# Attention's opening with sample work moved ahead of step 1, value fills from step 1, and later loads back from memory

## The chip, the cores and the metric

The kernel runs on one core of one Trainium2 chip. The metric is the device time of one execution in microseconds (us). A core has five engines that run at the same time, each through its own list of instructions: TensorE (PE: matmuls and transposes), VectorE (DVE), ScalarE (ACT), GpSimd (POOL) and SyncE (SP, which here only issues transfers). They wait for one another on semaphores. Transfers between the large memory and the on-chip buffers are issued from SP's queue (hardware queue, q1 in the profile) and POOL's queue (software queue, q0), and all run on the same 16 DMA engines.

## The reference, cut to what matters

One decoder layer for 1024 prompt tokens and 8 sample tokens. Between two feed-forward blocks stand an RWKV-7 branch and a differential attention with 4 heads of two maps each. What bears on the change is the attention:

```
def diff_attn_core(q, k, v, q_pos, k_pos, lam):
    s = jnp.einsum("bqhd,bkhd->bhqk", q, k).astype(F32) * (DA_QK ** -0.5)
    s = jnp.where(k_pos[None, :] <= q_pos[:, None], s, -jnp.inf)
    p = jax.nn.softmax(s, axis=-1).reshape(b, DA_HEADS, 2, tq, tk)
    w = p[:, :, 0] - lam * p[:, :, 1]
    return jnp.einsum("bhqk,bkhd->bqhd", w.astype(v.dtype), v)
...
        kp = cache_k[pt].reshape(n_past, 2 * DA_HEADS, DA_QK)
        vp = cache_v[pt].reshape(n_past, DA_HEADS, DA_V)
```

The prompt attends causally to itself, in blocks of 128 queries. Each of the 8 sample tokens attends to 2048 cached tokens, 16 pages of 128 tokens found through a page table, and to itself. A page of keys or values is 128 rows of 512 float32, 256 KB.

## The kernel before, in words

**Units.** Before attention, the input projection runs as 30 units (UNITS, numbers 0 to 29), 128 columns each: PE multiplies, DVE evicts the result from PSUM (L1922), ACT applies a sigmoid to a gate (L1382) and POOL saves it to memory (L931, gate_save). Into these units the sample's attention scores are woven: a *key group* f (0 to 31, four pages; group 4b to 4b+3 belongs to sample b) is loaded by SP into one of two slots of key_ring, and DVE multiplies it by the query (L1873) and sums it (L1877) into score_sums. GROUPS_OF says how many key groups each unit takes. SP issues the pages of group f after DVE's multiplication of group f-2 has freed the slot. When all 32 are done, DVE takes the maximum over each row (L1954), POOL the maximum over the partitions (L953).

**Steps.** Prompt attention is 27 steps (STEPS, numbers 0 to 26): step 0 takes the first query block with all 4 heads, steps 1 and 2 the second block with 2 heads each, then one head of one block per step. FIRST is 11: up to step 10 scores are made two steps ahead, later one. In a step PE makes scores of a later step (L2671), waits for this step's weights from DVE (the semaphore w_ready), transposes them (L2693), waits for ACT's copy of them (L1439), sums squares of the last output (L2677) and multiplies by the values (L2714). DVE's part of a step is to normalise the weights (L2023 to L2034; its end sets w_ready) and to find the maxima of a later step's scores (`maxima`, L2004 to L2007); ACT exponentiates (L1416).

**The sample's softmax** is woven in as three pieces on DVE (`sample_softmax`): piece 0 subtracts the maxima from the scores (L1965 to L1967), ACT exponentiates (`sample_exp`), piece 1 sums (L1970), PE sums over the partitions (`sample_sums`, L2635), piece 2 turns this into weights (L1974 to L1985).

**Fills.** A *fill* f (0 to 31) multiplies four value pages by the sample's weights on PE (L2647); FILL_STEP gives the step of each. Value pages go through a ring of three slots: SP issues the four pages of fill f when fill f-3 is done (the semaphore value_used), one page after the other, each with a page number read from the table (L701). The slot of f % 3 = 2 lies in tmp, so fill 2 also waits until all gates are saved. PE's order is fixed, so a fill whose pages have not landed holds up all that stands behind it. After the fourth fill of a sample its sum is moved, turned and added (`turn_sums`, `sample_out`).

**Loads back.** After the units, POOL issues the constants loop_masks (L954) and then 20 loads of 516 KB each, 10.57 MB together, of the RWKV operands kk, b_vec, k_new, r_mix and v_mix (L964). They are needed only after the last step. Their rows are 1032 float32 (4128 bytes) per partition, those of a value page 512 float32 (2048 bytes).

Of the kernel before, what the change touches and what calls it, by code (L numbers as in the profile page):

```python
# [11 lines left out]
AX = mybir.AxisListType.X  # L12
# [3 lines left out]
P = 128  # L16
# [3 lines left out]
NS = 8  # L20
# [16 lines left out]
PAGES = 16  # L37
# [94 lines left out]


UNITS = ZT + GT
GROUPS_OF = [0 if n == 0 else 2 if n in (15, 20, 26) else 1 for n in range(UNITS)]
HALF_OF = [n for n in range(UNITS) for _ in range(GROUPS_OF[n])]
PREP_AT = [4, 10, 16, 22]

# [90 lines left out]
def build(nc, A):  # L229

    ctx = ExitStack()
    with ctx:
        ev = Events(nc, ctx)
# [228 lines left out]
        AT_MERGE = AT_GATES + GT // 2  # L462
# [115 lines left out]
        BATCHES = [(0, range(0, 4)), (1, range(0, 2)), (1, range(2, 4))] + [(q, range(h, h + 1)) for q in range(2, 8) for h in range(HP)]  # L578
        STEPS = len(BATCHES)
        FIRST = 3 + 2 * HP  # L580
        FILL_STEP = [s for s in range(3, STEPS - 2) for _ in range(2 if s in (9, 11, 13, 14, 15, 18, 19, 20, 23, 24) else 1)]

        def heads_to(step):

# [191 lines left out]
        def _(pool):  # L776
# [132 lines left out]
            def spill_z(n):  # L909

                m = Z_ORDER[n]
                if m == 12 or 4 <= m < 8:
                    return
                pool.wait_ge(*ev.at("z_mixed", n + 1))
                if m == 13:
                    pool.wait_ge(*ev.at("z_act", 2))
                dst = gd_save if m == 13 else r_save[m] if m < 4 else v_save[m - 8]
                pool.dma_start(dst, ring[:, n % 2, :]).then_inc(ev[f"z_stored{n % 2}"], 16)

            for n in range(UNITS):  # L920
                p, s = n // 2, n % 2
                if n < ZT:
                    zm, z = z_place(n), T[:, s, :]
                    pool.wait_ge(*ev.at(f"psum_free{s}", AT_Z + p + 1))
                    pool.wait_ge(*ev.at("z_place", n + 1))
                    nc.gpsimd.tensor_tensor(zm[:, 1:NP], z[:, 0:NP - 1], z[:, 1:NP], ALU.subtract).then_inc(ev["z_diff"], 1)
                if 0 < n <= ZT:
                    spill_z(n - 1)
                if n >= ZT:
                    pool.wait_ge(*ev.at(f"gate_made{s}", p - ZPAIRS + 1))  # L930
                    pool.dma_start(g_save[n - ZT], T[:, s, :]).then_inc(ev[f"gate_saved{s}"], 16)  # L931
                for h in range(HP):
                    if PREP_AT[h] + 4 == n:
                        pool.wait_ge(*ev.at("cum_made", 2 * h + 2))
                        pool.dma_start(cum_save[h], cum).then_inc(ev["prep_stored"], 16)
                        pool.wait_ge(*ev.at("kk_made", h + 1))
                        pool.dma_start(kk_save[h], kkh).then_inc(ev["prep_stored"], 16)
                        pool.wait_ge(*ev.at("fac_made", h + 1))
                        nc.gpsimd.tensor_tensor(bh, bh, kkh, ALU.mult).then_inc(ev["b_made"], 1)
                        nc.gpsimd.tensor_tensor(kf[:, h, :], kf[:, h, :], fac, ALU.mult).then_inc(ev["kp_made"], 1)  # L940
                        pool.wait_ge(*ev.at("b_made", h + 1))
                        pool.dma_start(b_save[h], bh).then_inc(ev["prep_stored"], 16)
                        pool.wait_ge(*ev.at("kp_made", h + 1))
                        pool.dma_start(kp_save[h], kf[:, h, :]).then_inc(ev["prep_stored"], 16)
                if n == 16:
                    pool.wait_ge(*ev.at("side_moved", SIDE_AT["z_rows", 0, 0]))
                    pool.dma_start(A["shift_prompt"][0].rearrange("b (m p) -> (b m) p", p=P), zrow[0:ZT, :])\
                        .then_inc(ev["z_rows_stored"], 16)
                    pool.dma_start(A["shift_sample"][0].rearrange("b (m p) -> (b m) p", p=P), zrow[ZT:9 * ZT, :])\
                        .then_inc(ev["z_rows_stored"], 16)  # L950

            pool.wait_ge(*ev.at("s_max_part", 1))
            nc.gpsimd.partition_all_reduce(smax, smaxp, P, bass.bass_isa.ReduceOp.max).then_inc(ev["s_max_all"], 1)  # L953
            pool.dma_start(masks, A["const_table"][:, CONST_AT[LOOP_CONSTS]:NCONST]).then_inc(ev["masks_loaded"], 16)  # L954
            pool.wait_ge(*ev.at("unit_done0", AT_MERGE))
            pool.wait_ge(*ev.at("unit_done1", AT_MERGE))
# [1 line left out]
            pool.wait_ge(*ev.at("z_stored0", 16 * ring_before(ZT)))  # L958
            pool.wait_ge(*ev.at("z_stored1", 16 * ring_before(ZT + 1)))
            pool.wait_ge(*ev.at("z_rows_stored", 32))  # L960
            for dst, src, done in ((KKn, kk_save, "kk_back"), (Bf, b_save, "b_back"), (Kf, kp_save, "kp_back"),
                                   (Rf, r_save, "r_back"), (Vf, v_save, "v_back")):
                for h in range(HP):
                    pool.dma_start(dst[:, h, :], src[h]).then_inc(ev[done], 16)  # L964
# [140 lines left out]
        def _(act):  # L1105
# [312 lines left out]
            def decays(c):  # L1418
# [8 lines left out]
                    last = sc.activation(Pinv[:, h, :], CUMX[h][:, c, 1:C + 1], ACT.Exp, scale=-LOGDECAY)  # L1427
                last.then_inc(ev["ck_p"], 1)

            probs(0)  # L1430
            for step in range(STEPS):
                s, (qi, group) = (step + 1) % 2, BATCHES[step]
                if step + 1 < FIRST:
                    probs(step + 1)
                act.wait_ge(*ev.at("w_trans_lo", step + 1))
                if step >= FIRST:
                    act.wait_ge(*ev.at("w_trans_hi", step + 1 - FIRST))
                n = (qi + 1) * P * len(group)
                sc.activation(wT[s][:, 0:n], PSf[:, 4 * 512:4 * 512 + n], ACT.Copy).then_inc(ev["w_moved"], 1)  # L1439
                if FIRST <= step + 1 < STEPS:  # L1440
                    probs(step + 1)
                if step == STEPS - 2:
                    act.wait_ge(*ev.at("cum_back0", 16))
                    act.wait_ge(*ev.at("gate_saved0", 8 * GT))
                    act.wait_ge(*ev.at("gate_saved1", 8 * GT))
                    act.wait_ge(*ev.at("value_used", 4 * NS))
                    decays(0)
                act.wait_ge(*ev.at("o_done", step + 1))
                out = PS[:, 6, 0:len(group) * P]
                sc.activation(Q[:, group[0]:group[-1] + 1, qi * P:(qi + 1) * P], out.rearrange("p (h n) -> p h n", n=P), ACT.Copy)  # L1450
                if opens_block(step):
                    sums = PS[:, 5, 0:P] if qi < 3 else PS[:, 6, P:2 * P]
                    sc.activation(rmix[:, (qi - 1) * P:qi * P], sums, ACT.Copy, scale=1.0 / P).then_inc(ev["o_rows"], 1)
                if step == STEPS - 1:
                    sc.activation(rmix[0:96, qi * P:NP], PS[0:96, 6, P:2 * P], ACT.Copy, scale=1.0 / P)
                sc.activation(osq[:, 0:len(group) * P], out, ACT.Square).then_inc(ev["o_moved"], 1)
                if step == 0:
                    sample_exp()
                for b in range(NS):
                    if FILL_STEP[4 * b + 3] == step:  # L1460
                        act.wait_ge(*ev.at("value_used", 4 * b + 4))
                        sc.activation(osum, PS[:, 7, :], ACT.Copy).then_inc(ev["osum_moved"], 1)
# [136 lines left out]
        def _(dve):  # L1599
# [3 lines left out]
            def in_turn(instruction):  # L1603


                dve.drain()
# [301 lines left out]
            def unit_keys(h):  # L1908

                dve.wait_ge(*ev.at("side_moved", SIDE_AT["back", h, 2]))  # L1910
                in_turn(v.tensor_tensor(kkh, kkh, fac, ALU.mult).then_inc(ev["kk_made"], 1))

            q_diag(0)
            split(1, AT_Z)
            for n in range(UNITS):
                p, s = n // 2, n % 2
                c = AT_Z + p
                dve.wait_ge(*ev.at(f"unit_done{s}", c + 1))
                if p > ZPAIRS:
                    dve.wait_ge(*ev.at(f"gate_saved{s}", 16 * (p - ZPAIRS)))  # L1920
# [24 lines left out]
                for h in range(HP):  # L1945
# [3 lines left out]
                        inverse_norms(h)  # L1949
                    if PREP_AT[h] + 3 == n:  # L1950
                        unit_keys(h)

            smx = smaxp.rearrange("p (b m) -> p b m", b=NS)
            in_turn(v.tensor_reduce(smx, SC.rearrange("p (b g m) -> p b m g", b=NS, g=PAGES), AX, ALU.max)\  # L1954
                .then_inc(ev["s_max_part"], 1))

            def pages(a):

# [50 lines left out]
            def o_inverse(qi):  # L2009
# [3 lines left out]
                in_turn(v.tensor_scalar(rmix[:, b], rmix[:, b], 0.0, EPS, ALU.max, ALU.add))  # L2013
                in_turn(v.reciprocal(rmix[:, b], rmix[:, b]).then_inc(ev["o_inverse"], 1))

            maxima(0)
            maxima(1)
            sample_softmax(0)
            for step in range(STEPS):
                s, (qi, group) = (step + 1) % 2, BATCHES[step]  # L2020
                k, n, (_, total, inv, _) = len(group), (qi + 1) * P, softmax_columns(step)
# [14 lines left out]
                    maxima(step + 2)  # L2036
                if FIRST <= step + 1 < STEPS:
                    maxima(step + 1)
                if 0 < step < 3:
                    sample_softmax(step)  # L2040
                for b in range(NS):
                    if FILL_STEP[4 * b + 3] == step - 1:
                        sample_out(b)
# [316 lines left out]
        def _(pe):  # L2360
# [263 lines left out]
                    turn_rows(2 * HP - 1)  # L2624
            pe.wait_ge(*ev.at("side_moved", NSIDE))
            pe.wait_ge(*ev.at("psum_free0", AT_MERGE))
            pe.wait_ge(*ev.at("psum_free1", AT_MERGE))
            pe.wait_ge(*ev.at("k_back", 16))
            pe.wait_ge(*ev.at("q_back", 16))

# [46 lines left out]
                    mm(PS[32 * h:32 * h + 1, bank, at:at + P], K("ones")[:, 0:1], osq[:, i * P:(i + 1) * P], start=True, stop=True)  # L2677

            scores(0)
            scores(1)  # L2680
            for step in range(STEPS):
                s, (qi, group) = (step + 1) % 2, BATCHES[step]
# [2 lines left out]
                    scores(step + 2)  # L2685
                if FIRST <= step + 1 < STEPS:
                    scores(step + 1)
                if step == 2:
                    sample_sums()
                pe.wait_ge(*ev.at("w_ready", step + 1))  # L2690
                pe.wait_ge(*ev.at("w_moved", step))
# [382 lines left out]
```

## Time and profile before

| | us |
|---|---|
| median of 3 runs | 2707.53 |
| lowest, highest | 2707.19, 2708.59 |
| the profiled execution, whole | 2708.69 |
| its span on the core | 2707.0 |
| attention, first scores to the end of the last step's product | 1283.9 to 1485.0 |

The span is what the trace covers, and all moments below count from its start. PE is busy for 96% of the whole span, but the share hides that attention is different: the views by stretch below give busy time per engine inside it, with the clock that the throttle granted to TensorE (1.00 is 2.4 GHz, 0.50 is 1.2 GHz) and what the DMA engines moved. A row of the timeline is: start, duration, engine, line, operation, output <- input, and in brackets how long the engine sat idle before it and what ended that wait.

### The profile page before, as it was taken

The page shows a single profiled execution, that of the slowest core. Times are in us where ns is not written, and L with a number is a line of the kernel's source. Part 1 is how long each engine was busy: PE and PEld are TensorE (multiplying, and loading weights), DVE is VectorE, ACT ScalarE, POOL GpSimd, SP SyncE. Part 2 cuts the span into 40 slices and gives each one's busy share as a digit, 9 for nine tenths or more (in the row PEclk, how much of TensorE's full clock was granted, in tenths as well). Part 3 has the DMA queues.
Part 4 walks back from the last instruction along what each step waited for, and adds up shares of the span by engine and source line. Part 5 has one row for each costly group of instructions (what it writes and reads, how often), then busy time and mean ns, then how long its engine had stood idle before and what let it go on. Part 6 is the DMA issues. An engine that isn't in the chain of part 4 may idle for free.

```text
span 2707.0 us, 55005 instructions
## 1 busy us (share of the span) xinstructions
PE 2595.5 (96%) x22506; PEld 2464.0 (91%) x22506; DVE 1709.3 (63%) x2054; ACT 802.3 (30%) x1306; POOL 592.4 (22%) x534
## 2 busy tenths in 40 slices
PE   7999999999999999998787999979999999999998
PEld 7999999999999999998344899869999999999998
DVE  5877777422484588677766778675487677763223
ACT  6333333111211222332444233221343333331012
POOL 2333332100010232111100655220023333320000
PEclk8999999999999999999799999979999999999999
DMA  5233332751323545667876000043323333235411
GB/s 196 73 116 98 110 107 64 272 182 55 102 95 106 157 142 171 220 203 251 287 223 184 30 27 28 20 147 109 125 75 111 106 99 112 73 106 203 153 47 71
DMA packets 293398, 342.12 MB, mean 126 GB/s; under 512 B 22324, under 2 KB 217744, under 8 KB 293024
## 3 DMA queue, kind: packets, MB, share of 16 engines
q1 hardware_dynamic: 252960, 189.42, 23.6%
q0 software_dynamic: 40000, 149.17, 15.2%
q8 instruction: 176, 2.88, 0.4%
q14 instruction: 70, 0.57, 0.1%
q10 hardware_dynamic: 192, 0.07, 0.0%
HBM read 254.32 MB, written 84.28 MB: 125 GB/s over the span
## 4 chain that ended last, share of the span: by engine, by line
PE 86%; DVE 7%; issue 2%; SPq 1%; DMA 1%; ACT 1%; DVEq 0%; POOL 0%; ACTq 0%
PE ps L2384 42%; PE ps L2512 31%; PE ps L2752 1%; PE ps L2767 1%; PE ps L2772 1%; PE ps L2429 1%; PE ps L2714 1%; DVE small L2006 1%; SPq L700 1%; PE ps L2671 1%; PE ps L2604 1%; DMA q_rot<-q_save 1%; PE ps L2647 1%; PE ps L2799 1%; SPq L701 1%
## 5 line engine op out<-in xcount | busy, mean ns | idle before, releaser
L2384 PE MATMUL ps<-h,w_hi 128*128 128x344 f32 x2112 | 506.4, 323 | 0.0
L2384 PEld LDWEIGHTS ps<-h,w_hi 128*128 128x128 f32 x2112 | 361.9, 188 | 17.4 <-issue 16.7
L2384 PE MATMUL ps<-h,w_lo 128*128 128x344 f32 x1056 | 336.7, 319 | 0.0
L1766 DVE SCALAR_TENSOR_TENSOR x_res<-ps,x_res 128x1032 f32<-128x1032 f32 x48 | 59.2, 1233 | 322.0 <-PE ps L2384 322.0
L2512 PE MATMUL ps<-t,w_hi 128*128 128x258 f32 x1408 | 259.3, 285 | 0.0
L1182 ACT ACTIVATE w_hi<-w_stage 128x512 fp32r<-128x512 f32 x252 | 157.6, 627 | 315.9 <-PE ps L2512 279.8
L2512 PE MATMUL ps<-t_one,w_hi 128*128 128x258 f32 x1280 | 234.3, 284 | 3.1 <-issue 2.5
L2512 PEld LDWEIGHTS ps<-t,w_hi 128*128 128x128 f32 x1408 | 219.9, 191 | 0.0
L1708 DVE TENSOR_TENSOR tmp<-tmp,ps 128x516 f32<-128x516 f32 x210 | 145.4, 692 | 106.8 <-PE ps L2512 93.7
L1677 DVE TENSOR_TENSOR w_lo<-w_stage,w_hi 128x512 fp32r<-128x512 f32 x252 | 192.0, 762 | 22.7 <-ACT w_hi L1182 0.4
L2512 PEld LDWEIGHTS ps<-t_one,w_hi 128*128 128x128 f32 x1280 | 198.9, 190 | 3.4 <-issue 3.4
L2512 PE MATMUL ps<-t,w_lo 128*128 128x258 f32 x704 | 199.9, 284 | 0.0
L2384 PEld LDWEIGHTS ps<-h,w_lo 128*128 128x128 f32 x1056 | 198.3, 188 | 0.0
L2512 PE MATMUL ps<-b,w_hi 128*128 128x258 f32 x1056 | 192.7, 283 | 0.0
L2512 PE MATMUL ps<-t_one,w_lo 128*128 128x258 f32 x640 | 181.2, 283 | 0.0
L2512 PE MATMUL ps<-h,w_hi 128*128 128x258 f32 x960 | 174.8, 283 | 1.4 <-ACT tmp L1206 0.8
L2512 PEld LDWEIGHTS ps<-b,w_hi 128*128 128x128 f32 x1056 | 163.3, 189 | 0.0
L809 POOL TENSOR_TENSOR w_stage<-w_stage 128x512 f32<-128x512 f32 x42 | 76.7, 1827 | 344.5 <-DVE w_lo L1677 336.6
L2512 PEld LDWEIGHTS ps<-h,w_hi 128*128 128x128 f32 x960 | 148.3, 189 | 1.9 <-issue 1.8
L2512 PE MATMUL ps<-b,w_lo 128*128 128x258 f32 x528 | 149.1, 282 | 0.0
L1192 ACT ACTIVATE w_hi<-w_stage 128x1024 fp32r<-128x1024 f32 x49 | 51.7, 1056 | 285.1 <-PE ps L2384 266.5
L2512 PE MATMUL ps<-h,w_lo 128*128 128x258 f32 x480 | 135.4, 282 | 0.0
(551 smaller groups left out, 6161.1 us busy)
## 6 DMA issues: line engine op xcount, KB each, us to landing
w_stage<-in_ffn_up SPq DMA_DIRECT2D x176, 256.0 KB, 3.0
key_ring<-in_cache_k SPq DMA_DIRECT2D x128, 256.0 KB, 3.0
value_ring<-in_cache_v SPq DMA_DIRECT2D x88, 256.0 KB, 3.0
w_stage<-in_w_in SPq DMA_DIRECT2D x84, 256.0 KB, 3.4
w_stage<-in_ffn_down SPq DMA_DIRECT2D x80, 256.0 KB, 3.3
g_save<-g_ring POOLq DMA_DIRECT2D x32, 516.0 KB, 4.8
g_save<-g_kept POOLq DMA_DIRECT2D x32, 516.0 KB, 4.4
x_res<-x_save POOLq DMA_DIRECT2D x6, 2064.0 KB, 9.3
```

Of the source, the lines that this page charges most:

```text
L700: page = sp.value_load(ptab[0:1, at], min_val=0, max_val=N_PHYS - 1)
L701: sp.dma_start(slot, cache[ds(page, 1)].rearrange("a t n -> (a t) n")).then_inc(ev[done], 16)
L809: nc.gpsimd.tensor_tensor(A12, A12, A11, ALU.subtract).then_inc(ev[of(m, "sum_made")], 1)
L1182: sc.activation(op_slot(whi, n), RAW[i], ACT.Copy).then_inc(ev[of(m, "op_high")], 1)
L1192: sc.activation(whi[b], stg[b], ACT.Copy).then_inc(ev[f"w_high{b}"], 1)
L1677: in_turn(v.tensor_tensor(op_slot(wlo, n), RAW[n % NPROD], op_slot(whi, n).bitcast(F32), ALU.subtract) .then_inc(ev[of(m, "op_low")], 1))
L1708: in_turn(v.tensor_tensor(halved(out), halved(x), region(bank), ALU.add).then_inc(ev[of(m, "ps_read")], 1))
L1766: in_turn(v.scalar_tensor_tensor(ch3(xm), dense[s], 0.5, ch3(xm), ALU.mult, ALU.add) .then_inc(ev[f"psum_free{s}"], 1))
L2006: in_turn(v.tensor_reduce(top, scores, AX, ALU.max))
L2384: last = mm(dense[s][:, j], w[w0][:, k0 + k, :], column(r, k, slice(j * CH, (j + 1) * CH)), start=(k == 0 and n == 0), stop=(k == nk - 1 a ...
L2429: last = mm(dense[s][:, j], w[s][:, k, :], r[:, k, j * CH:(j + 1) * CH], start=(k == 0 and n == 0), stop=(k == KT - 1 and n == 2))
L2512: last = mm(PS[:, bank + c, 0:QUART], w[:, k, :], moving[:, x, k, b], start=(opens and k == 0 and a == 0), stop=(k == 3 and a == 2), skip_ ...
```

## The change

In words:

1. GROUPS_OF: unit 29 has no key group, unit 27 has two instead of one. Groups 29 and 30 are now multiplied in unit 27, group 31 in unit 28. DVE takes the row maximum at the head of unit 29, ahead of that unit's eviction, and POOL the maximum over partitions in unit 29, ahead of the save of the last gate.
2. sample_softmax: piece 0 ahead of the maxima of steps 0 and 1, piece 1 behind them, piece 2 in step 0 (before: piece 0 behind those maxima, piece 1 in step 1, piece 2 in step 2). sample_exp stands ahead of the first exponentials, and PE's sample_sums in step 0 instead of step 2.
3. FILL_STEP: sample b has one fill in step 3b+1, two in step 3b+2 and one in step 3b+3, from step 1 to step 24. Before, fills ran from step 3 to step 24: one a step, and two in steps 9, 11, 13, 14, 15, 18, 19, 20, 23 and 24.
4. POOL issues the 20 loads back only when step 5 has been transposed (w_trans_lo reaches 6). Before, it did so right after the maximum over partitions.
5. PE waits for the eviction of unit 29 only ahead of the scores of step 1, no longer ahead of those of step 0.

```
-GROUPS_OF = [0 if n == 0 else 2 if n in (15, 20, 26) else 1 for n in range(UNITS)]
+GROUPS_OF = [0 if n in (0, UNITS - 1) else 2 if n in (15, 20, 26, 27) else 1 for n in range(UNITS)]
...
-        FILL_STEP = [s for s in range(3, STEPS - 2) for _ in range(2 if s in (9, 11, 13, 14, 15, 18, 19, 20, 23, 24) else 1)]
+        FILL_STEP = [3 * b + k for b in range(NS) for k in (1, 2, 2, 3)]
...
+                if n == UNITS - 1:
+                    pool.wait_ge(*ev.at("s_max_part", 1))
+                    nc.gpsimd.partition_all_reduce(smax, smaxp, P, bass.bass_isa.ReduceOp.max).then_inc(ev["s_max_all"], 1)
...
-            pool.wait_ge(*ev.at("s_max_part", 1))
-            nc.gpsimd.partition_all_reduce(smax, smaxp, P, bass.bass_isa.ReduceOp.max).then_inc(ev["s_max_all"], 1)
...
+            pool.wait_ge(*ev.at("w_trans_lo", 6))
             for dst, src, done in ((KKn, kk_save, "kk_back"), (Bf, b_save, "b_back"), (Kf, kp_save, "kp_back"),
...
+            sample_exp()
             probs(0)
...
-                if step == 0:
-                    sample_exp()
...
+                if n == UNITS - 1:
+                    in_turn(v.tensor_reduce(smx, SC.rearrange("p (b g m) -> p b m g", b=NS, g=PAGES), AX, ALU.max)
+                            .then_inc(ev["s_max_part"], 1))
                 dve.wait_ge(*ev.at(f"unit_done{s}", c + 1))
...
+            sample_softmax(0)
             maxima(0)
             maxima(1)
-            sample_softmax(0)
+            sample_softmax(1)
...
-                if 0 < step < 3:
-                    sample_softmax(step)
+                if step == 0:
+                    sample_softmax(2)
...
-            pe.wait_ge(*ev.at("psum_free1", AT_MERGE))
...
             scores(0)
+            pe.wait_ge(*ev.at("psum_free1", AT_MERGE))
             scores(1)
...
-                if step == 2:
+                if step == 0:
                     sample_sums()
```

**How the order moves.** On DVE, from the end of the units to the opening of attention, before:

```order
L1922 TENSOR_TENSOR tmp<-ps,rstd_mix 128x1032
L1873 TENSOR_TENSOR kq_prod<-key_ring,rstd 128x2048
L1877 TENSOR_REDUCE score_sums<-kq_prod 128x32
L1954 TENSOR_REDUCE rstd<-score_sums 128x64
L2004 TENSOR_TENSOR ps<-ps,const 128x1024
L2006 TENSOR_REDUCE rstd<-ps 128x8
L2007 TENSOR_SCALAR rstd<-rstd 128x8
L2004 TENSOR_TENSOR ps<-ps,const 128x4x128
L2006 TENSOR_REDUCE rstd<-ps 128x4
L2007 TENSOR_SCALAR rstd<-rstd 128x4
L1965 TENSOR_TENSOR rstd<-rstd,s_self 128x64
L1966 TENSOR_TENSOR score_sums<-score_sums,rstd 128x1024
```

and now (line numbers are up to 5 higher; L1921 is the row maximum, L1966 to L1968 are piece 0):

```order
L1874 TENSOR_TENSOR kq_prod<-key_ring,rstd 128x2048
L1878 TENSOR_REDUCE score_sums<-kq_prod 128x32
L1921 TENSOR_REDUCE rstd<-score_sums 128x64
L1927 TENSOR_TENSOR tmp<-ps,rstd_mix 128x1032
L1966 TENSOR_TENSOR rstd<-rstd,s_self 128x64
L1967 TENSOR_TENSOR score_sums<-score_sums,rstd 128x1024
L1968 TENSOR_TENSOR s_self<-s_self,rstd 128x64
L2005 TENSOR_TENSOR ps<-ps,const 128x1024
L2007 TENSOR_REDUCE rstd<-ps 128x8
L2008 TENSOR_SCALAR rstd<-rstd 128x8
L2005 TENSOR_TENSOR ps<-ps,const 128x4x128
```

The last key group and the maximum went ahead of the last eviction, and piece 0 went ahead of the first maxima.

On PE, in steps 1 and 2 (from the transposes of step 1 to the scores made in step 3), before:

```order
L2693 MATMUL ps<-const,probs 128x128 x4
L2677 MATMUL ps<-o_squares,const 1x128 x4
L2714 MATMUL ps<-w_trans_105,v_tok 128x128 x4
L2671 MATMUL ps<-k_rot,q_rot 128x384 x2
L2635 MATMUL ps<-rstd,const 128x64
L2693 MATMUL ps<-const,probs 128x128 x4
L2677 MATMUL ps<-o_squares,const 1x128 x2
L2714 MATMUL ps<-w_trans_106,v_tok 128x128 x4
L2671 MATMUL ps<-k_rot,q_rot 128x384 x2
```

and now:

```order
L2695 MATMUL ps<-const,probs 128x128 x4
L2678 MATMUL ps<-o_squares,const 1x128 x4
L2716 MATMUL ps<-w_trans_105,v_tok 128x128 x4
L2648 MATMUL ps<-value_ring,s_weights 4x512 x4
L2672 MATMUL ps<-k_rot,q_rot 128x384 x2
L2695 MATMUL ps<-const,probs 128x128 x4
L2648 MATMUL ps<-value_ring,s_weights 4x512 x4
L2648 MATMUL ps<-tmp,s_weights 4x512 x4
L2678 MATMUL ps<-o_squares,const 1x128 x2
L2716 MATMUL ps<-w_trans_106,v_tok 128x128 x4
L2672 MATMUL ps<-k_rot,q_rot 128x384 x2
```

Three fills (L2648) entered these two steps, and the partition sum (L2635) left for step 0.

## Rows read from the trace of the kernel before

**Rows 1.** The page: the span.

```profile
span 2707.0 us, 55005 instructions
```

**Rows 2.** By stretch: PE, PEld, DVE, ACT, POOL busy; clock, DMA share, GB/s.

```profile
1284.00:1320.00 36.00, 21.92 (x97) 14.06 (x97) 29.36 (x52) 14.27 (x53) 11.55 (x22) 0.55 0.99 384
1320.00:1365.00 45.00, 38.16 (x248) 19.49 (x252) 30.13 (x69) 20.52 (x61) 0.00 (x0) 0.91 0.68 202
```

**Rows 3.** Timeline of SP and PE at attention's opening: the query load, the first scores.

```profile
1268.00 0.51 SPq L721 DMA_DIRECT2D q_rot<-q_save  x1
...
1283.89 3.38 PE L2671 MATMUL ps<-k_rot,q_rot 64*128 64x128 f32 x24 [7.29 <-DMA q_rot<-q_save]
```

**Rows 4.** Timeline of DVE and POOL: last key groups, the two maxima.

```profile
1259.71 2.29 DVE L1873 TENSOR_TENSOR kq_prod<-key_ring,rstd 128x2048 f32<-128x2048 f32 x1
...
1277.96 2.29 DVE L1873 TENSOR_TENSOR kq_prod<-key_ring,rstd 128x2048 f32<-128x2048 f32 x1
...
1282.71 1.99 DVE L1954 TENSOR_REDUCE rstd<-score_sums 128x64 f32<-128x1024 f32 x1
...
1288.12 0.54 POOL L953 PARTITION_ALL_REDUCE rstd<-rstd  x1 [8.24 <-issue]
```

**Rows 5.** Timeline of DVE: pieces 0, 1, 2 begin; weights of steps 1 and 3.

```profile
1291.59 1.23 DVE L1966 TENSOR_TENSOR score_sums<-score_sums,rstd 128x1024 f32<-128x1024 f32 x1
...
1300.56 0.69 DVE L2029 TENSOR_TENSOR probs<-probs 128x512 f32<-128x512 f32 x1
...
1303.40 2.00 DVE L1970 TENSOR_REDUCE rstd<-score_sums 128x64 f32<-128x1024 f32 x1
...
1310.59 0.22 DVE L1974 TENSOR_TENSOR rstd<-rstd,ps 128x64 f32<-128x64 f32 x1
...
1318.24 0.62 DVE L2034 SCALAR_TENSOR_TENSOR probs<-probs,small 128x384 f32<-128x384 f32 x1
```

**Rows 6.** Timeline of PE in steps 2 and 3.

```profile
1307.08 1.65 PE L2671 MATMUL ps<-k_rot,q_rot 64*128 64x384 f32 x4
...
1309.15 1.06 PE L2693 MATMUL ps<-const,probs 128*128 128x128 f32 x4
...
1311.42 2.08 PE L2714 MATMUL ps<-w_trans,v_tok 128*128 128x128 f32 x8
...
1318.91 0.90 PE L2693 MATMUL ps<-const,probs 128*128 128x128 f32 x3 [3.83 <-DVE probs L2034]
...
1322.50 1.89 PE L2647 MATMUL ps<-value_ring,s_weights 128*4 128x512 f32 x8
```

**Rows 7.** Fills: what ended waits before L2647; timeline of SP and PE, steps 11, 15.

```profile
  DMA value_ring<-in_cache_v: 5.2, 5
  DMA tmp<-in_cache_v: 3.2, 3
...
1364.39 1.90 PE L2647 MATMUL ps<-value_ring,s_weights 128*4 128x512 f32 x16
...
1388.40 3.61 SPq L701 DMA_DIRECT2D tmp<-in_cache_v  x4
...
1394.43 1.04 PE L2647 MATMUL ps<-tmp,s_weights 128*4 128x512 f32 x8 [0.86 <-DMA tmp<-in_cache_v]
```

**Rows 8.** DMA queues: packets, MB, engine share in 1328-1330, 1292-1294, 576-578; a load's landing.

```profile
q1 hardware_dynamic: 266, 0.49, 84.2%
...
q0 software_dynamic: 140, 0.53, 70.4%
q1 hardware_dynamic: 124, 0.24, 32.0%
...
q0 software_dynamic: 172, 0.71, 89.6%
q1 hardware_dynamic: 172, 0.08, 14.1%
...
v_mix<-v_save POOLq DMA_DIRECT2D x4, 516.0 KB, 20.1
```

More of the change, by code:

```diff
@@ L1911, in unit_keys @@
                 in_turn(v.tensor_tensor(kkh, kkh, fac, ALU.mult).then_inc(ev["kk_made"], 1))
+            smx = smaxp.rearrange("p (b m) -> p b m", b=NS)
             q_diag(0)
@@ L1951, in _ @@
                         unit_keys(h)
-            smx = smaxp.rearrange("p (b m) -> p b m", b=NS)
-            in_turn(v.tensor_reduce(smx, SC.rearrange("p (b g m) -> p b m g", b=NS, g=PAGES), AX, ALU.max)\
-                .then_inc(ev["s_max_part"], 1))
             def pages(a):
```

## The prediction

> **What bounds the kernel now.** Attention fills 1283.9 to 1485.0 us of the 2707.0 us span [rows 1, 3]; the change touches only it and the 25 us ahead of it, so I read the busy time by stretch first. In the opening (1284 to 1320) DVE is busy 29.4 of 36 us, PE 21.9, and the clock granted is 0.55, so nearly all of PE's work runs at 1.2 GHz; from 1320 to 1365 PE is busy 38.2 of 45 us at a clock of 0.91 [rows 2]. So the opening belongs to DVE, the rest to PE. Then the timelines, for what ends PE's waits. The first scores start at 1283.89 behind the query load, issued at 1268.00 [rows 3]. PE's last long wait in the opening, 3.83 us, ends with the weights of step 3 at 1318.9 [rows 6]. Third, the fills: eight waits on value pages, 8.4 us together [rows 7]. They show a second limit. Fill 17's four pages are issued from 1388.40 and its product starts at 1394.43: 6.0 us from a free slot to use, and SP issues a page in 1.09 us (3.61 us from the first issue to the end of the fourth, so 1.09 apart), hence a fill in 4.36 us at best. The last view is the DMA queues in windows of 2 us [rows 8]: alone, SP's queue moves 0.49 MB in 2 us, that is 240 GB/s, the rate of 1 MB per 4.36 us.
>
> **Units 27 to 29: no gain, none lost.** SP issues group 31's pages when group 29's multiplication is over, at 1262.0 [rows 4], and that row has nothing ahead of it that moves. So the keys come no sooner, and the query load behind them in SP's queue keeps its 1268.0. What moves is DVE work: groups 30 and 31 (2.3 + 2.3 us each) and the maximum (1.99) run back to back from 1264.5 with two evictions of 1.3 between them: 1264.5 + 4.7 + 1.3 + 4.7 + 2.0 = 1277.2. Unit 29's eviction slips by some 0.6 us; what waits for it is the scores of step 1, after 1284, so it costs nothing. POOL's maximum ended at 1288.66 and its input was ready at 1284.7 [rows 4]: 4.0 us, now 1277.2 to 1281.2. The last gate's save waits behind it, about 2 us later; who waits is fill 2's pages, not used before step 2. Bound for the first scores: 1 us sooner (less beside the query load) to 0; I take 0, the query load is what they wait for.
>
> **The opening: DVE's gain is handed back.** Piece 0 (1.9 us from 1291.3) [rows 5] goes into the wait for the queries, piece 1 (2.0 us) takes its place: step 0 is unmoved, its weights ready at 1296.0 as before. Piece 2 (1310.6 to about 1315.8, 5.2 us, [rows 5]) now stands between the weights of steps 0 and 1: those of step 1, at 1301.25 before [rows 5], come at 1306.5. From there PE needs transposes, ACT's copy, squares and product, 4.35 us as in step 2 (1309.15 to 1313.50) [rows 6]: 1310.9. Then fill 0 at the slow clock (1.9 us) and the scores for step 4 (1.65 us) [rows 6]: 1314.5. DVE waits for these, needs 1.7 us for their maxima (1308.8 to 1310.5, just ahead of piece 2) and 3.0 us for the output's inverse and the weights of step 3 (from piece 2's end at 1315.8 to 1318.86) [rows 5]: 1319.2, where it was 1318.9 [rows 5]. PE meanwhile does step 2 with fills 1 and 2 (3.8 us at the slow clock) and is some 5 us behind at step 3, less once its clock is up, with four fills done by step 3's end where it had one. I put the whole opening at +1 us in time and three fills ahead (bounds: -2 if the denser PE gets the full clock sooner, +4 if not).
>
> **The fills: more of them early, against the same rate.** Every three steps now take four fills. In steps 3 to 10 a step took 4 to 6 us, so four fills want to run in about 15 us, and SP needs 17.4 us to issue them. Fill 0 ends at 1312.9; SP then issues without a pause, and fill 6 lands at about 1333. At the full rate fill 14, the last of step 11, lands at 1333 + 8 x 4.36 = 1368; before, step 11 ended its second fill (the eleventh, not the fifteenth) at 1366.3 [rows 7]. So even undisturbed the value stream alone is 1.7 us behind there, plus 1 us for the fill itself: +2.7.
>
> **The loads back: the term that decides.** 10.57 MB are issued at step 5's transposes, near 1331, into a stretch where SP's queue is wanted at its full 240 GB/s. Before, they ran from 1289 to 1319 (the last four land 20.1 us after 1298 to 1300) [rows 8], when at most one fill's pages were in flight. What two full queues do is in the trace: from 576 to 578 they move 172 packets each, 0.71 and 0.08 MB, since packets of POOL's queue are 4128 bytes and those of the weights 512; the packets alternate. From 1292 to 1294, with the last value pages of the opening beside the first loads back, it is 140 against 124 packets, 0.53 against 0.24 MB [rows 8]. So value pages get 120 GB/s, not 240, while POOL's queue gets 265, for 10.57 / 0.265 = 40 us. In these 40 us 4.8 MB of pages arrive, 4.6 fills instead of 9.2. Fill 14 then lands at 1333 + 38 + (8 - 4.4) x 4.36 = 1387, its product ends at 1388, 22 us behind 1366.3. The bounds of this term: an equal share by bytes (192 GB/s each of the 384 in [rows 2]) gives 5.5 us per fill and 1377, 12 us behind; no loss at all gives 1369, 2.7 behind. I take the 22, because the row of 1292 shows this very pair of transfers.
> The Trainium skill, "DMA: Bandwidth & Descriptors", on arbitration, says that an engine round-robins between queue rows packet by packet, one packet being some 9 to 17 descriptors; that speaks against this change. A value page and a load back both give 8 rows to each engine, so by it value pages would get a third, 128 GB/s, and fill 14 would be 1 us sooner than by the row.
>
> **Behind step 11.** From step 12 the change has 17 fills where before had 21: 4 x 0.95 = 3.8 us less on PE (a fill is 1.04 at the full clock) [rows 7]. The steps are 6.5 to 8 us there and want at most 1.33 fills each, so SP keeps up, and waits such as the 0.86 before fill 17 [rows 7] go; I count 2 us of the 8.4. Against it, long waits on pages in steps 6 to 11 would leave PE at 1.2 GHz there, as in the opening [rows 2]; PE's work between the waits then takes up to twice as long, partly inside them: 0 to +5 us, I take +1.5. The end of attention: +22 - 3.8 - 2 + 1.5 = +17.7, with the opening already in the moment of fill 6. Nothing behind attention moves: the loads back are done near 1371, a hundred us before they are wanted. The profiled execution, 2708.7, would be 2726.4; on the median of 2707.5 that is **2725.2**.
>
> **Rivals.**
> *A. Pages starve, as above* (0.70). Term bounds: 12 to 24 us at step 11, so +7 to +24 at the end: 2714 to 2732.
> *B. The loads back slip in* (0.16). SP's queue alone leaves some 145 of 384 GB/s, and if value pages kept at least half by bytes, the loss at step 11 is 3 to 12 us, and the 5.8 us behind it give most of that back: -3 to +6, middle +2, 2709.5. For it: DMA share in 1320 to 1365 is only 0.68 [rows 2]. Against it: the 0.24 MB of 1292. To this case belongs that the change doesn't do what it says, since key pages do not come sooner.
> *C. Faster* (0.14). The mechanism is the even spread: value pages hold 4.36 us a fill beside the loads back, all 8.4 us of waits on pages vanish, and a PE that never waits long keeps 2.4 GHz where [rows 2] show 0.91. That gives 2.7 - 3.8 - 8.4 + 2 (waits that arise early) = -7.5, with clock up to -10: 2697 to 2701, I take 2700. It decides at about 215 GB/s for SP's queue in 1331 to 1371; below that fill 14 is over 5 us late and eats it.
>
> **Chances.** What a measurement here can tell from no change is about 0.2%, 5.4 us: 2702 to 2713. From A nearly all is slower; of B some 0.03 is slower and 0.13 same; C is faster by nine parts in ten. Slower 0.73, same 0.14, faster 0.13. The range for 8 in 10 reaches down to the middle of B and up past A's +24 by what a slow clock may add: 2704 to 2734.
>
> **What would show it.** In the profile after: the first scores still at 1283.9; step 3's weights near 1319; the queues from 1331 to about 1371 with SP's at 0.24 MB in 2 us and POOL's at 0.53; waits of PE before L2648 on value pages of well over 8.4 us, nearly all before 1390, and after it almost none; attention ending near 1503. If SP's queue keeps 0.45 MB in 2 us beside POOL's, the decisive term is wrong, and B or C holds. If step 3's weights come at 1315 or sooner, the opening was mis-walked.

## The result and the profile after

The changed kernel takes **2723.5 us** in the median of five runs (2720.8 to 2726.1), beside 2707.5 for the kernel before: a ratio of **1.0059, 95% interval 1.0045 to 1.0074**, so 16 us slower. The forecast was 2725.2.

The profiled execution has a span of 2721.4 us, against 2707.0 [rows 1]. Everything ahead of attention stands some 2.5 us earlier on its clock: the first eviction that the change leaves in its place (L1927 here, L1922 before) starts at 1254.55 us instead of 1257.06. So I count from the start of the first scores, 1280.53 here and 1283.89 before [rows 3]. Attention then lasts to 1499.15, the end of its last output product, which is 218.6 us, where it lasted 201.1. The whole loss lies there: from attention's end to the span's it is 1222.2 us here and 1222.0 before.

The same stretches as in [rows 2] and two more, of the kernel after (columns: busy time of PE, PEld, DVE, ACT, POOL, then granted clock, DMA share, GB/s):

```profile
span 2721.4 us, 55005 instructions
...
1284.00:1320.00 36.00, 23.00 (x130) 12.47 (x128) 28.56 (x54) 15.43 (x58) 0.00 (x0) 0.75 0.37 122
1320.00:1365.00 45.00, 22.36 (x124) 9.56 (x124) 18.73 (x42) 10.48 (x33) 10.59 (x20) 0.79 0.99 368
1365.00:1400.00 35.00, 29.60 (x201) 17.08 (x201) 20.84 (x50) 15.09 (x40) 0.00 (x0) 0.93 0.75 242
1400.00:1485.00 85.00, 72.19 (x481) 41.69 (x478) 62.95 (x125) 39.59 (x84) 0.00 (x0) 0.96 0.54 165
```

From 1320 to 1365 PE does 124 matmuls in 22.4 us, where it did 248 in 38.2; the DMA engines, 0.99 busy in the opening and 0.68 here before, are now 0.37 busy in the opening and 0.99 here. The POOL column holds the 20 issues. Two lines of the DMA queues say what that does, the first pair from 1342 to 1344, the last line from 1368 to 1370, when the loads back are over (packets, MB, share of 16 engines):

```profile
q0 software_dynamic: 146, 0.54, 67.2%
q1 hardware_dynamic: 146, 0.27, 35.7%
...
q1 hardware_dynamic: 413, 0.76, 102.7%
```

SP's queue has 135 GB/s beside POOL's and 380 as soon as it is alone (with some pages in arrears). The price is in PE's timeline, the fills that wait and fill 14:

```profile
1325.57 2.13 POOL L966 DMA_DIRECT2D kk<-kk_save  x4 [43.92 <-PE ps L2695]
...
1332.95 1.89 PE L2648 MATMUL ps<-value_ring,s_weights 128*4 128x512 f32 x8 [7.00 <-DMA value_ring<-in_cache_v]
1341.79 1.04 PE L2648 MATMUL ps<-value_ring,s_weights 128*4 128x512 f32 x8 [3.80 <-DMA value_ring<-in_cache_v]
1357.48 1.89 PE L2648 MATMUL ps<-value_ring,s_weights 128*4 128x512 f32 x8 [5.15 <-DMA value_ring<-in_cache_v]
1365.32 1.89 PE L2648 MATMUL ps<-value_ring,s_weights 128*4 128x512 f32 x8 [5.95 <-DMA value_ring<-in_cache_v]
...
1385.25 1.04 PE L2648 MATMUL ps<-tmp,s_weights 128*4 128x512 f32 x8
```

Three of the four long waits end with a fill at 1.89 us, nearly twice the 1.04 that it takes at 2.4 GHz: PE came out of the wait at 1.2. In all, PE's own waits on pages are 23.0 us (waits: total, times, longest), of before 2.2:

```profile
PE ps L2648 <- DMA value_ring<-in_cache_v: 22.4, 5, 7.0
PE ps L2648 <- DMA tmp<-in_cache_v: 0.6, 2, 0.3
...
PE ps L2647 <- DMA value_ring<-in_cache_v: 1.3, 2, 0.7
PE ps L2647 <- DMA tmp<-in_cache_v: 0.9, 1, 0.9
```

The chain of waits names PE for 85% of the whole span and the value pages for 1%. That looks like nothing, but 1.1% of 2721 us is 30 us: two stretches of 10.92 and 18.39 us, from 1330.82 and 1346.89, both while the loads back run (the chain counts the transfer's time there, not only PE's idle time). A share of the whole span hides what the same chain shows in a window.

### The profile page after: what moved, and what is told of

Same layout as the page of the kernel before. It is cut to its first block, busy times and chain, and to the rows that moved or that the text cites. A ratio compares the mean times of both kernels' runs of the same rounds, so it can differ in the third digit from the quotient of the medians.

```text
span 2721.4 us, 55005 instructions
## 1 busy us (share of the span) xinstructions
PE 2591.4 (95%) x22506; PEld 2458.6 (90%) x22506; DVE 1710.0 (63%) x2054; ACT 802.3 (29%) x1306; POOL 592.4 (22%) x534
## 4 chain that ended last, share of the span: by engine, by line
PE 85%; DVE 9%; DMA 3%; issue 1%; ACT 1%; SPq 1%; DVEq 0%; POOL 0%; ACTq 0%
PE ps L2386 41%; PE ps L2514 30%; PE ps L2754 1%; DMA value_ring<-in_cache_v 1%; PE ps L2769 1%; PE ps L2774 1%; PE ps L2431 1%; PE ps L2716 1%; DVE small L2007 1%; PE ps L2606 1%; PE ps L2801 1%; PE ps L2672 1%; PE ps L2648 1%; DVE kq_prod L1874 1%; PE ps L2809 1%
## 5 line engine op out<-in xcount | busy, mean ns | idle before, releaser
L2514 PE MATMUL ps<-t,w_lo 128*128 128x258 f32 x704 | 200.1, 284 | 0.0
L2514 PE MATMUL ps<-b,w_hi 128*128 128x258 f32 x1056 | 192.7, 283 | 0.0
```

The source lines that it names most:

```text
L2514: last = mm(PS[:, bank + c, 0:QUART], w[:, k, :], moving[:, x, k, b], start=(opens and k == 0 and a == 0), stop=(k == 3 and a == 2), skip_ ...
```

## Experiments: which part costs

The change has three parts: (1) the loads back behind step 5's transposes; (2) the table of fills; (3) key groups and sample softmax earlier. Theory S: all is (1), through the shared engines. The rival: the table costs or gains by itself.

**The wait that makes the loads back late, taken out of the change (e1), and put alone on the kernel before (e2).**

```diff
-            pool.wait_ge(*ev.at("w_trans_lo", 6))    # e1: out of the changed kernel
+            pool.wait_ge(*ev.at("w_trans_lo", 6))    # e2: into the kernel before
```

> The changed kernel without POOL's new wait, so the 20 loads back start right behind the maximum over partitions, as before the change; fills and sample softmax stay as changed. Theory S (value pages starve beside the loads back): the loads are done by about 1317, when SP has just begun to refill value slots; PE's waits on value pages before step 12 fall from about 22 us to under 6, fill 14 is used near 1366 instead of 1386, and the time is 2704 to 2710 us. Rival F (the new table of fills is the cost, since four fills in three short steps want more than SP can issue): the time stays at 2716 or more, and the waits on pages stay above 12 us.

Measured: 2707.7 us, 1.0001 (0.9992 to 1.0011) of before; attention 201.6 us.

> The kernel before with one line of the change: POOL waits for the transposes of step 5 ahead of the loads back. Theory S: from 1328 to 1368 value pages get 0.27 MB in 2 us instead of 0.49, 20 us of their stream are lost, the old fills had at most 2 us to spare between steps 11 and 15, so the time is 2722 to 2728 us with the last fill of step 15 near 1412. Rival F: the old table spares enough, 2708 to 2713 us.

Measured: 2722.7 us, 1.0055 (1.0038 to 1.0071); attention 214.3 us. The waits of PE on pages, of the first and of the second kernel:

```profile
PE ps L2647 <- DMA value_ring<-in_cache_v: 7.9, 3, 4.1
PE ps L2647 <- DMA tmp<-in_cache_v: 1.8, 1, 1.8
...
PE ps L2648 <- DMA value_ring<-in_cache_v: 10.5, 4, 6.6
PE ps L2648 <- DMA tmp<-in_cache_v: 5.5, 2, 4.1
```

One wait on POOL, which is 22% busy, carries the loss: 15.8 us taken away, 15.0 put on. In the traces, attention is 17.0 us shorter without it (218.6 and 201.6), and 13.3 of these are PE's waits on pages (23.0 and 9.7); the other 3.7, of which fills at the lower clock behind a wait are a part, were not taken apart. The 9.7 us of waits left in the first kernel are more than the 6 that were expected; they are the table's, as the next runs show.

**The table, with the loads late and with them early.**

```diff
-        FILL_STEP = [3 * b + k for b in range(NS) for k in (1, 2, 2, 3)]
+        FILL_STEP = [s for s in range(3, STEPS - 2) for _ in range(2 if s in (9, 11, 13, 14, 15, 18, 19, 20, 23, 24) else 1)]
```

> The changed kernel with the old table of fills (from step 3, two in ten of the steps); the late loads back stay. Theory S: as slow as the changed kernel or up to 4 us slower, 2721 to 2728 us, since the value stream starts later into the same 40 us of shared engines. Rival F: the table was the cost, 2708 to 2713 us.

Measured: 2718.3 us, 1.0042 (1.0025 to 1.0059); PE's waits on pages 18.0 us. That is below theory S's range and above the rival's.

> The changed kernel with both undone, the old table of fills and the early loads back: what is left are the key groups one unit sooner and the sample softmax ahead of step 1. Theory S and the walk of the opening: step 3's weights within 2 us of where they were, no starving, 2703 to 2708 us. If the opening's piece 2 in step 0 costs what it saves, it is 2707.5 to within 1 us.

Measured: 2703.9 us, 0.9986 (0.9976 to 0.9995); PE's waits 2.6 us, attention 197.3. So the table costs 5.2 us with the loads late and 3.8 with them early, and part (3) alone gains 3.8. By medians: -3.8 for the earlier softmax and key groups, +3.8 for the table, +15.8 for the loads, together +15.8, beside the +16.0 that was measured. The two small parts stand only just clear of the scatter: e4's interval against before allows a gain of 1.4 to 6.5 us, and the single runs of e1 (2706.5 to 2709.6) and e4 (2700.7 to 2708.4) overlap. For the table the traces say the same as the times: PE's waits on pages are 5.0 us shorter without it when the loads are late, and 7.1 when they are early. The loads' part is 14.4 to 15.8 in the three pairs, so it hardly depends on the table.

## Experiments: is it the place, the bytes or the burst

**Later, and only half of them.**

```diff
-            pool.wait_ge(*ev.at("w_trans_lo", 6))
+            pool.wait_ge(*ev.at("w_trans_lo", 17))           # e6
...
+                    if done == "kp_back" and h == 2:         # e7, in the loop of the loads
+                        pool.wait_ge(*ev.at("w_trans_lo", 6))
```

> The changed kernel with POOL waiting for the transposes of step 16 (w_trans_lo at 17) instead of step 5. Theory S with the step length in it: from step 16 a step takes 8 us and wants 1.33 fills, one in 6 us, while a fill takes 8 us beside the loads back; in 41 us 6.8 fills are wanted, 4.9 arrive and two are in the ring ahead, so most of the loss is covered: 2708 to 2716 us. Rival (the loads back cost the same wherever they run beside value pages): 2720 us or more.

Measured: 2718.5 us, 1.0046 (1.0029 to 1.0063), between the two ranges: the cost is smaller there than at step 5, but two thirds of it are left (10.8 us over e1, of 15.8). From 1422 to 1424, 25 us after POOL's first issue, the queues read

```profile
q0 software_dynamic: 141, 0.52, 65.4%
q1 hardware_dynamic: 141, 0.26, 34.7%
```

and the last fill to wait in that stretch waits 6.79 us, at 1439.31. I had thought that the longer steps there leave SP room. In e1 a step takes 7.4 us from step 16 to 21 and wants 1.33 fills, one in 5.6 us: that leaves SP 1.2 us a fill at its full rate of 4.36, and none at a third of the engines.

> The changed kernel with the wait for step 5's transposes put in front of the second ten of the 20 loads back; the first ten start right behind the maximum. Theory S: the shared stretch is 20 us instead of 41 and loses 2.3 fills instead of 4.7, so fill 14 is used 10 us sooner than in the changed kernel: 2711 to 2717 us, midway between the early loads (2707.7) and the changed kernel (2723.5). Rival T (a threshold: any loads back after step 5 spoil PE's clock or its order for good): 2720 us or more.

Measured: 2713.1 us, 1.0017 (1.0007 to 1.0026): 5.4 us over e1 for half of the bytes, where all cost 15.8. PE's waits on pages are 12.6 us, 2.9 over e1, where the whole burst adds 13.3. So the cost grows faster than the bytes. That the ring of pages takes the first part of a burst would explain it; no run tests that.

**Paced.** The same 20 loads in the same kernel, one behind each of the steps 5 to 24:

```diff
-            pool.wait_ge(*ev.at("w_trans_lo", 6))
+            i = 0
...
                 for h in range(HP):
+                    pool.wait_ge(*ev.at("w_trans_lo", 6 + i))
                     pool.dma_start(dst[:, h, :], src[h]).then_inc(ev[done], 16)
+                    i += 1
```

> The change, with GpSimd's 20 loads back issued one behind each of the steps 5 to 24 instead of all behind step 5. The bytes and the work are the same. While both queues run the engines move some 400 GB/s (0.79 MB in 2 us in the changed kernel), with the pages alone 245. A step of 5 us then has to bring one fill (1.05 MB) and one load (0.53 MB), 1.6 MB, which 400 GB/s bring in 4 us. Theory S (the cost is a burst that takes two thirds of the engines for 41 us while the fills are needed at their full rate): PE's waits on pages fall from 23 us to 2-8 and the time to 2706-2713. Rival B (any loads back during attention cost by their bytes, wherever they stand: 10.6 MB at 245 GB/s would be 43 us of engine time, of which the changed kernel paid 15.8): 2718-2724 as in the kernel with the loads at step 16.

Measured: **2707.1 us, 1.0000 (0.9991 to 1.0009)**; attention 200.1 us. Below, its row for 1320 to 1365, two of the twenty issues, and the queues' totals from 1330 to 1460:

```profile
1320.00:1365.00 45.00, 32.37 (x214) 16.32 (x213) 25.81 (x60) 16.29 (x51) 3.37 (x7) 0.92 0.90 299
...
1352.35 0.54 POOL L967 DMA_DIRECT2D b_vec<-b_save  x1 [4.94 <-PE ps L2697]
1358.39 0.54 POOL L967 DMA_DIRECT2D b_vec<-b_save  x1 [5.50 <-PE ps L2697]
...
q1 hardware_dynamic: 14291, 26.01, 61.5%
q0 software_dynamic: 2598, 9.53, 21.3%
...
PE ps L2650 <- DMA value_ring<-in_cache_v: 8.4, 3, 6.3
PE ps L2650 <- DMA tmp<-in_cache_v: 1.8, 1, 1.8
```

The same bytes inside attention cost nothing that can be measured against e1 (2707.1 and 2707.7), and PE's waits are again those of e1 (10.2 and 9.7 us). 9.5 MB of loads and 26.0 MB of pages passed in 130 us. So neither the bytes nor a place inside attention cost by themselves; the burst does, which for 41 us in a row holds SP's queue below what the fills want (where the burst stands matters some: 10.8 us at step 16, 15.8 at step 5). The rival by bytes is out.

**The size of the rows.** The engines take turns by packets, so smaller rows on POOL's queue should leave more to SP's. (The counts that later waits on these loads expect are raised to match.)

```diff
-                    pool.dma_start(dst[:, h, :], src[h]).then_inc(ev[done], 16)
+                    for q in (slice(0, HALF), slice(HALF, NT)):        # e5; e10: four quarters
+                        pool.dma_start(dst[:, h, q], src[h][:, q]).then_inc(ev[done], 16)
```

> The changed kernel with each load back cut into two of 128 x 516, so that POOL's queue carries packets of 2064 bytes beside value pages' 2048; bytes and moment are the same. Theory S, with packets of the two queues taken in turn: value pages get half of the bytes, near 0.38 MB in 2 us instead of 0.27, the loads back take some 55 us instead of 41, fill 14 is used about 10 us sooner than in the changed kernel, and the time is 2710 to 2717 us. Rival Q (the queues share by bytes or by a fixed weight, whatever the packet): 0.27 MB in 2 us as in the changed kernel and 2721 to 2726 us.

Measured: 2728.8 us, 1.0075 (1.0058 to 1.0092). No gain at all: outside what either theory had expected, above it. The lines of the queues, 1342 to 1344, show why the premise failed:

```profile
q0 software_dynamic: 157, 0.52, 67.5%
q1 hardware_dynamic: 150, 0.27, 37.9%
```

The share is the old one. POOL's queue moves 3.3 kB a packet: a transfer brings each engine 8 rows of 2064 bytes, 16.5 kB, and with one small packet at its end that fits four packets of 4128 bytes (4/5 of 4128 is 3.30), not eight of 2064 (8/9 of it would be 1.83). Two rows had been put in one packet. The row size was not the packet size, so the experiment changed nothing but the number of issues; attention is 219.5 us, as in the changed kernel (218.6). The two medians are 5.3 us apart, and the intervals overlap. Of the 6.8 us between the two profiled spans 2.9 lie ahead of attention, 0.9 in it and 3.0 behind it, so the loads' share of the engines does not explain them; the cause stays open.

> The change, with the loads back written as 80 transfers of 128 rows of 1032 bytes instead of 20 of 4128. In the kernel with 40 transfers of 2064-byte rows the trace has GpSimd's queue at 3.3 kB a packet (five packets for the 16.5 kB that a transfer brings to each engine, one of them small), not at 1.8: two rows went in one packet, and the two queues still took turns packet by packet, 0.25 to 0.14 MB in 1 us. Theory K (turns by packets, and the software queue fills a packet up to some 4.1 kB): here 3 packets for 8.3 kB, so 2.75 kB a packet on average; 240 packets an engine instead of 180, the shared stretch grows from 41 to some 52 us, at 2.75 to 1.8 kB; PE's waits on pages 23-30 us, time 2724-2733. Rival R (a packet is a row, as for the pages of the other queue): under 1 kB a packet, the pages get over 60 per cent of the bytes, PE's waits 5-15 us, time 2710-2720.

Measured: 2721.2 us, 1.0055 (1.0041 to 1.0068); attention 215.7 us; PE's waits on pages 20.9 us. The queues, 1342 to 1344, and the 80 issues' first group:

```profile
q0 software_dynamic: 159, 0.43, 60.0%
q1 hardware_dynamic: 159, 0.29, 42.4%
...
1325.53 8.60 POOL L967 DMA_DIRECT2D kk<-kk_save  x16 [44.01 <-PE ps L2696]
```

0.43 MB in 159 packets is 2.70 kB each, near the 2.75 of theory K (two of 4128 and a small one for 8.3 kB), and the two queues again have 159 packets each. Rival R, a packet to a row, is out. But the time is 3 us below K's range, and so are the waits (K: 23 to 30); the interval overlaps that of the changed kernel. The shared stretch did grow, to the 52 us of K (1325.5 to 1377), at 0.29 MB in 2 us for SP's queue instead of 0.27. What K left out is the start: POOL needs 43 us to issue 80 transfers at 0.54 us, and from 1326 to 1334 its queue brings 1.11 MB and SP's 1.30, where the changed kernel has 1.64 and 0.91. Whether this start is the whole of the difference was not tested.

**The table by measured rates.** Loads early, the changed kernel's opening, and fills that begin at step 2 and are spread with the aim that none is wanted sooner than SP's rate allows:

```diff
-        FILL_STEP = [3 * b + k for b in range(NS) for k in (1, 2, 2, 3)]
+        FILL_STEP = [2, 3, 4, 4, 6, 7, 8, 8, 10, 11, 11, 12, 13, 13, 14, 14, 15, 16, 16, 17, 18, 18, 19, 19, 20, 20, 21, 22, 23, 23, 24, 24]
-            pool.wait_ge(*ev.at("w_trans_lo", 6))
```

> The early loads back with another table of fills, one a step or less until step 10 and two in twelve of the later steps (from step 2 to step 24), with the sample softmax of the change. Theory S: fills should never be wanted faster than one in 4.4 us nor all come early; the waits on value pages fall below 2 us and PE has fewer long gaps: 2698 to 2704 us, faster than before. Rival: the table is worth nothing beyond the old one, 2703 to 2706 us.

Measured: **2700.8 us, 0.9976 (0.9967 to 0.9986)**: 7 us faster than the kernel before, 23 than the changed one. Its row and its waits:

```profile
1320.00:1365.00 45.00, 37.23 (x256) 19.86 (x256) 32.19 (x74) 21.82 (x63) 0.00 (x0) 1.00 0.72 209
...
PE ps L2647 <- DMA value_ring<-in_cache_v: 4.1, 4, 1.7
```

The waits are 4.1 us where under 2 were expected. In this execution PE keeps the full clock from 1320 to 1365, as in no other profiled one here, and attention takes 192.7 us. But it is one of the best three of its ten runs (2695.9 to 2696.7, with a mean granted clock of 0.980 to 0.981 over the whole run); the other seven took 2700.5 to 2705.1 at 0.976 to 0.977, so the row shows the kernel at its best and not at its median. Over e4 the gain is 3.2 us, and the two intervals against before overlap: that this table beats the old one is likely but not shown. Whether the 3.2 us come from fills in steps 2 to 4, from fewer in late steps or from the clock was not taken apart.

## Why the prediction was right, and where its steps were not

**The decisive term held, for its reason.** Fill 14's product ends 105.8 us behind the first scores (1386.29 - 1280.53); before, step 11 ended 82.4 behind them: +23.4, where the working had +22. SP's queue had 0.27 MB in 2 us beside POOL's 0.54, for the 0.24 and 0.53 forecast, and the shared stretch ran from 1326 to 1367, 41 us, for 40. The rule that was weighed beside it, from the Trainium skill, "DMA: Bandwidth & Descriptors", on arbitration in its section "Queues, rings and completion order" (turns between queues at packet boundaries, with some 9 to 17 descriptors in a packet), gives a third to the pages here, as an estimate with a descriptor to a row and as many in a turn of either queue; and a third it was. But that count is not what the queues showed: in e5 both queues had rows of 2 kB, which by it would give halves, and the split stayed two to one. What fits all three kernels (whole, half and quarter rows) is a packet of about 4.1 kB on POOL's queue and of one 2 kB row on SP's.

The size at step 11 hides two errors that cancel in part. With the loads early the changed table alone is 6.8 us behind there (e1, below), so the late loads account for 16.6 of the 23.4; the working had 2.7 and 19.3.

**Behind step 11** it was -5.8 for the -4.3 of the sum; together +17.5 for attention, against +17.7. That close an agreement is partly luck, for two terms besides that of the loads were mis-sized, and a third can't be told from scatter:

- *The opening, +1.* The weights of step 3 end 34.5 us behind the first scores (1315.00 - 1280.53), before 35.0: -0.5. The moment itself, 1315.00, is the one that the prediction had named as the sign of a mis-walked opening, but here everything stands 3.4 us earlier. In the four other kernels whose program is the same up to step 5 (e5, e6, e9, e10) it is 34.2 to 35.8 us, that is -0.7 to +0.8, so one trace can't tell -0.5 from +1. What was wrong is the clock: the working went through step 3's work at 1.2 GHz, and the rows show the higher clock from about 1309 on:

```profile
1307.29 1.67 PE L2648 MATMUL ps<-value_ring,s_weights 128*4 128x512 f32 x8
1308.88 0.92 PE L2672 MATMUL ps<-k_rot,q_rot 64*128 64x384 f32 x4
...
1309.85 0.43 DVE L2005 TENSOR_TENSOR ps<-ps,const 128x256 f32<-128x256 f32 x1 [2.28 <-PE ps L2672]
...
1314.38 0.62 DVE L2036 SCALAR_TENSOR_TENSOR probs<-probs,small 128x384 f32<-128x384 f32 x1
```

The scores take 0.92 us, where they took 1.65 [rows 6], and DVE has them that much sooner; in the four others just named they take 0.92 to 0.98. In e1, with the same fills and the loads early, the scores behind fill 0 still take 1.65 (at 1311.74), so the rise does not follow from the early fills alone; what sets it stays open. The mean clock of the stretch, 0.75 here and 0.55 before, is no measure of it: e6 and e9, with the rise at the same place, have 0.65 and 0.66.
- *The waits of before, 8.4 us* [rows 7], of which 2 were to vanish. That view adds each wait for PE's matmul and for its weight load; PE alone had 2.2 us, in the lines above. So rival C's main gain, all 8.4, was never there.
- *The fill table undisturbed, +2.7 at step 11.* In e1 fill 14 ends at 1372.03, 89.2 us behind its first scores at 1282.81: +6.8. The table's waits are 9.7 us even with the loads early, and its whole cost 3.8. Fills in steps 1 to 3 buy nothing if SP's rate of 4.36 us a fill has to carry the next ones.

**Smaller steps.** The keys came no sooner, as forecast, and the first scores stand 0.85 us nearer to the eviction that was taken as the mark above (0 to 1 forecast). The maximum over partitions is used by DVE at 1280.50, 5.6 us after its input (1272.82 + 2.07), where the working had 4.0; piece 0 starts then and ends at 1282.3, in the time of the first scores, so it costs nothing. Rival B fell with the 0.27 MB; it would have needed half by bytes.

## What to carry over

A transfer that nobody waits for is not free if it shares the engines with a stream that is wanted at its full rate: compare the two queues' packets and bytes in a window where both are full, and the share follows. Before moving a burst, ask whether it can be spread over the steps; here one load a step cost nothing and twenty at once cost 15 us. And read waits by engine before counting them: a view that adds the matmul's and the weight load's waits can count the same idle time twice.

## What the runs showed of the hardware

- Two full queues take turns packet by packet, whatever the packets hold: 146 to 146, 141 to 141, 159 to 159 in 2 us (157 to 150 in e5), 0.54 to 0.27 MB with whole rows. POOL's queue puts several rows of a strided transfer into one packet of about 4.1 kB (two of 2064, four of 1032 bytes, worked out from 3.3 and 2.7 kB a packet on average); SP's keeps one row of 2048.
- With both queues full the engines moved 0.78 to 0.81 MB in 2 us with whole and half rows, but 0.72 with quarter rows; SP's queue alone, with pages in arrears, moved 0.76.
- SP's queue alone moves 0.49 MB in 2 us [rows 8] when its issues of 1.09 us set the pace, and 0.76 when pages are in arrears: the 240 GB/s are SP's issue rate, not the engines'.
- The moment at which attention starts varies from 1279.3 to 1285.8 us between profiled executions of kernels whose work ahead of it is nearly the same (1282.81 and 1279.98 in e1 and e4, which differ only behind it). A single span can't tell 3 us.
